# A value product with seven block products instead of eight for one of two expert pairs, its extra sums on POOL and DVE

## The reference, cut to what matters

```python
def peer_ffn(hn, w_q, sub_keys, u, v):      # hn (256, 1024); u, v (16384, 1024)
    ...                                      # top-16 experts of 8 heads per token: eidx, gate
    act = gelu(einsum('td,ted->te', xb, u[eidx])) * gate
    return einsum('te,ted->td', act, v[eidx])
```

## Time and profile before

| | us |
|---|---|
| median of 3 runs | 2187.45 (2179.83 to 2189.59) |
| the profiled execution's own time | 2180.91 |
| its span, first to last instruction | 2179.1 |
| value stage, layer 0 / layer 1 | 348.4 / 348.6 |
| mean granted TensorE clock | 0.986 of full speed |

### The profile page before, as it was taken

The page is one execution under the profiler, slowest core; times in us unless marked ns, Lnnn a source line. Parts: engine busy times, 40 slices in busy tenths (PEclk is TensorE's granted clock), DMA queues, the critical chain, the costliest instruction groups (busy, mean ns, idle before and its releaser), DMA issues.

```text
span 2179.1 us, 45295 instructions
## 1 busy us (share of the span) xinstructions
PE 2089.8 (96%) x14548; PEld 1896.7 (87%) x14548; DVE 1441.2 (66%) x3050; ACT 1314.5 (60%) x3093; POOL 388.9 (18%) x342
## 2 busy tenths in 40 slices
PE   7889899999999999999998998999999999999997
PEld 7889499999999988888788895999999998888886
DVE  5764349778887666666567633496778886666665
ACT  5530145699999655555565302556999995555554
POOL 0312007632222100000003120175322220000000
PEclk9999999999999999999999998999999999999999
DMA  5320244444444555555552102444444445555554
GB/s 210 116 78 1 97 155 165 165 171 157 156 168 157 176 192 192 192 192 192 192 189 97 59 1 98 173 174 166 162 155 170 156 155 191 194 193 192 192 192 184
DMA packets 47464, 338.82 MB, mean 155 GB/s; under 512 B 5649, under 2 KB 5777, under 8 KB 6929
## 3 DMA queue, kind: packets, MB, share of 16 engines
q1 hardware_dynamic: 47376, 337.73, 43.2%
HBM read 336.66 MB, written 1.05 MB: 155 GB/s over the span
## 4 chain that ended last, share of the span: by engine, by line
PE 85%; DVE 9%; ACT 2%; DMA 2%; issue 1%; DVEq 0%; SPq 0%; ACTq 0%; PEldq 0%
PE ps L815 11%; PE ps L814 11%; PE ps L816 11%; PE ps L784 10%; PE ps L786 9%; PE ps L785 9%; PE ps L687 3%; PE ps L407 2%; PE ps L408 2%; PE ps L409 2%; PE ps L550 2%; PE ps L564 1%; PE ps L794 1%; PE ps L795 1%; PE ps L423 1%; DVE expert_lo L1320 1%
## 5 line engine op out<-in xcount | busy, mean ns | idle before, releaser
L784 PE MATMUL ps<-h_t_hi,expert_hi 128*128 128x256 f32 x2048 | 591.3, 289 | 12.3 <-DVE expert_lo L1686 8.5
L785 PE MATMUL ps<-h_t_lo,expert_hi 128*128 128x256 f32 x2048 | 578.5, 282 | 0.0
L786 PE MATMUL ps<-h_t_hi,expert_lo 128*128 128x256 f32 x2048 | 578.2, 282 | 0.0
L1869 POOL TENSOR_TENSOR expert_lo<-w_ring,expert_hi 128x512 fp32r<-128x512 f32 x204 | 289.8, 1429 | 772.1 <-ACT expert_hi L975 770.4
L784 PEld LDWEIGHTS ps<-h_t_hi,expert_hi 128*128 128x128 f32 x2048 | 391.6, 191 | 15.6 <-ACT big L980 8.2
L814 PE MATMUL ps<-expert_hi,act_hi 128*128 128x512 f32 x1024 | 398.4, 389 | 0.0
L815 PE MATMUL ps<-expert_lo,act_hi 128*128 128x512 f32 x1024 | 398.4, 389 | 0.0
L816 PE MATMUL ps<-expert_hi,act_lo 128*128 128x512 f32 x1024 | 398.3, 389 | 0.0
L785 PEld LDWEIGHTS ps<-h_t_lo,expert_hi 128*128 128x128 f32 x2048 | 392.0, 191 | 0.0
L786 PEld LDWEIGHTS ps<-h_t_hi,expert_lo 128*128 128x128 f32 x2048 | 391.6, 191 | 0.0
L975 ACT CAST expert_hi<-w_ring 128x512 fp32r<-128x512 f32 x512 | 308.0, 614 | 98.3 <-PE ps L786 83.7
(11 more groups left out here) (294 smaller groups left out, 3279.2 us busy)
## 6 DMA issues: line engine op xcount, KB each, us to landing
w_ring<-u_t SPq DMA_DIRECT2D x128, 1024.0 KB, 4.8
w_ring<-v_t SPq DMA_DIRECT2D x128, 1024.0 KB, 4.8
w_ring<-w_in SPq DMA_DIRECT2D x32, 1024.0 KB, 4.8
w_ring<-w_q SPq DMA_DIRECT2D x16, 1024.0 KB, 4.8
w_ring<-w_out SPq DMA_DIRECT2D x8, 1024.0 KB, 4.8
big<-xconst SPq DMA_DIRECT2D x2, 1666.0 KB, 9.5
w_ring<-keys SPq DMA_DIRECT2D x2, 1024.0 KB, 4.7
big<-rows SPq DMA_DIRECT2D x2, 576.0 KB, 11.2
```

The source lines that it names most:

```text
L784: pe.matmul(o, w_hi[:, c, :], HTH[:, d, :], start=d == 0, stop=False)
L785: pe.matmul(o, w_hi[:, c, :], HTL[:, d, :], start=False, stop=False)
L786: mm = pe.matmul(o, w_lo[:, c, :], HTH[:, d, :], start=False, stop=d == DC - 1)
L1869: pool.tensor_tensor(EL[:, m % 4, :], RING[:, m // 4, (m % 4) * 512:(m % 4 + 1) * 512], EH[:, m % 4, :].bitcast(F32), ALU.subtract).then_i ...
```

## The change

Bodies 1 to 30 of each layer treat their first expert pair as a product of 2x2 blocks: the activations as A (token tile x expert tile), the values as B11, B12, B21, B22 (expert tile x column half). A Strassen-type scheme (Winograd's form) computes it with seven block products p1 to p7 instead of eight. Each is three matmuls of 128x512, as before. The second pair stays as it was and is now called c0 to c3. Body 0 and body 31 of each layer keep the old form.

The scheme needs sums of the operands: four 128x128 sums of activations (`ASUM`, POOL), and four 128x512 sums of values: T1 = B12 - B11, T2 = T3 + B11 and T4 = B21 - T2 on POOL, T3 = B22 - B12 on DVE. POOL also makes the low of the four activation sums (`ASL`). Highs are still ACT's and all other lows DVE's. There are now six buffers for highs and lows of values (four `EH`, two in `h_t_hi`, free in this stage).

The products p2, p3, p4 are added into banks 0, 1 and 2; p1, p5, p6 and p7 have banks 4 to 7. After the last body `fold` combines them with eight DVE additions of 128x512, before the four additions of before.

The loads are cut into four of 512 KB per body, each with its own semaphore. Load 0 (B11, B12) now waits for T2 of the body before, load 1 (B21, B22) for T4.

PE:

```diff
+            def v_product(name, j, bank, a_hi_t, a_lo_t, start):
+                pe.wait_ge(v_lo, v_at(name, j))
+                o, s = PS[:, bank, :], v_slot(name)
+                pe.matmul(o, a_hi_t, VH[s], start=start, stop=False, skip_group_check=True)
+                pe.matmul(o, a_hi_t, VL[s], start=False, stop=False, skip_group_check=True)
+                pe.matmul(o, a_lo_t, VH[s], start=False, stop=True, skip_group_check=True).then_inc(v_done, 1)
...
+            def v_body(j, first):
+                pe.wait_ge(a_lo, 4 * j + 1)
+                v_product("p1", j, 4, A11H, A11L, first)
+                pe.wait_ge(a_lo, 4 * j + 3)
+                v_product("p2", j, 0, A2H[:, a12], A2L[:, a12], False)
+                pe.wait_ge(s_lo, j)
+                v_product("p3", j, 1, ASH[:, s4], ASL[:, s4], False)
+                v_classic("c0", j, 0, 0)
+                v_product("p7", j, 7, ASH[:, s3], ASL[:, s3], first)
+                v_product("p6", j, 6, ASH[:, s2], ASL[:, s2], first)
+                v_product("p5", j, 5, ASH[:, s1], ASL[:, s1], first)
+                v_classic("c1", j, 0, 1)
+                v_product("p4", j, 2, A2H[:, a22], A2L[:, a22], False)
+                pe.wait_ge(a_lo, 4 * j + 4)
+                v_classic("c2", j, 1, 0)
+                v_classic("c3", j, 1, 1)
```

ACT, one body (`b_high` waits for its buffer and makes one high of 512; `left(name)` waits until PE has done that product of the body before):

```diff
+                left("p1", 1)
+                act.copy(A11H, acts(0, 0, P)).then_inc(a_hi, 1)
+                act.wait_ge(v_landed[0], 16 * (j + 1))
+                b_high("p1", B11, j, first)
+                act.wait_ge(s_made, 3 * j)
+                left("p5", 1)
+                act.copy(ASH, ASUM).then_inc(s_hi, 1)
+                act.wait_ge(v_landed[1], 16 * (j + 1))
+                b_high("p2", B21, j, first)
+                left("c1", 6)
+                act.copy(AH[:, 0, :], acts(2, 0, S)).then_inc(a_hi, 1)
+                left("p4", 1)
+                act.copy(A2H, acts(1, 0, S)).then_inc(a_hi, 1)
+                b_high("p3", B22, j, first)
+                act.wait_ge(v_landed[2], 16 * (j + 1))
+                b_high("c0", RING[:, 1, 0:512], j, first)
+                act.wait_ge(t3_made, j)
+                b_high("p7", T3, j, first)
+                act.wait_ge(t_made, 3 * j - 1)
+                b_high("p6", T2, j, first)
...
+                b_high("p5", T1, j, first)
+                b_high("c1", RING[:, 1, 512:1024], j, first)
+                act.wait_ge(t_made, 3 * j)
+                b_high("p4", T4, j, first)
...
```

DVE, one body (`b_low` waits for the high and makes one low of 512):

```diff
+                a_low(1, A11L, 0, 0, P, A11H)
+                b_low("p1", B11, j)
+                b_low("p2", B21, j)
+                dve.tensor_tensor(T3, B22, B12, ALU.subtract).then_inc(t3_made, 1)
+                a_low(2, AL[:, 0, :], 2, 0, S, AH[:, 0, :])
+                a_low(3, A2L, 1, 0, S, A2H)
+                b_low("p3", B22, j)
...
+            def fold():
...
+                dve.wait_ge(folded, 1)
+                plus(T1, PS[:, 6, :])
+                plus(x11, PS[:, 4, :])
+                plus(x22, PS[:, 5, :])
...
```

POOL, one body:

```diff
+                    pool.tensor_copy(ATOP, both)
+                    pool.tensor_tensor(s3, acts(0, 0), acts(0, 1), ALU.subtract)
+                    pool.tensor_tensor(s1, acts(0, 1), acts(1, 1), ALU.add).then_inc(s_made, 1)
+                    pool.wait_ge(s_made, 3 * j - 2)
+                    pool.tensor_tensor(s2, s1, ATOP[:, 0, :], ALU.subtract).then_inc(s_made, 1)
+                    pool.wait_ge(s_made, 3 * j - 1)
+                    pool.tensor_tensor(s4, ATOP[:, 1, :], s2, ALU.subtract).then_inc(s_made, 1)
+                    pool.wait_ge(v_landed[0], 16 * (j + 1))
...
+                    pool.tensor_tensor(T1, B12, B11, ALU.subtract).then_inc(t_made, 1)
+                    pool.wait_ge(s_hi, j)
+                    pool.tensor_tensor(ASL, ASUM, ASH.bitcast(F32), ALU.subtract).then_inc(s_lo, 1)
+                    pool.wait_ge(t3_made, j)
+                    pool.tensor_tensor(T2, T3, B11, ALU.add).then_inc(t_made, 1)
+                    pool.wait_ge(v_lo, v_at("p3", j))
+                    pool.wait_ge(t_made, 3 * j - 1)
+                    pool.tensor_tensor(T4, B21, T2, ALU.subtract).then_inc(t_made, 1)
```

SP:

```diff
+                with sp.Fori(2, N_BODY) as j:
+                    sp.wait_ge(t_made, 3 * j - 4)
+                    load_v(0, j)
+                    sp.wait_ge(t_made, 3 * j - 3)
+                    load_v(1, j)
+                    sp.wait_ge(v_lo, v_at("c1", j - 1))
+                    load_v(2, j)
+                    sp.wait_ge(v_lo, v_at("c3", j - 1))
+                    load_v(3, j)
```

More of the change, by code:

```diff
@@ L363, in _ @@
                     sp.wait_ge(*u_lows_made(4 * i + 3, N_BODY - 1, False))
[L364 to L368, removed]
+                    for c in range(2):
+                        load_v(2 * i + c, 0)
+                for c in range(4):
+                    sp.wait_ge(v_lo, 2 * c + 2)
+                    load_v(c, 1)
+                with sp.Fori(2, N_BODY) as j:
[7 more added lines that the diff above has]
+                    load_v(3, j)
                 for i in range(2):
-                    sp.wait_ge(v_lo, 252 + 4 * i)
+                    sp.wait_ge(v_lo, V_ALL - 4 + 4 * i)
                 first_loads(L - 1)
@@ L891, in _ @@
                 for m in range(8):
[L892 to L896, removed]
+                    v_half(m, 0, True, 0)
+                v_body(1, True)
+                with pe.Fori(2, N_BODY - 1) as j:
+                    v_body(j, False)
+                for m in range(8):
+                    v_half(m, N_BODY - 1, False, V_ALL - 8)
+                pe.wait_ge(v_done, V_ALL)
                 pe.sem_inc(arrived, 1)
@@ new lines, in a_split, with b_high @@
+                if first and e == 2:
+                    act.wait_ge(u_mul, 2 + 128 - LATE)
+                if e >= 2:
+                    act.wait_ge(v_done, 2 * e - 2 if first else V_ALL - 10 + 2 * e)
+                elif not first:
+                    act.wait_ge(v_done, v_at(("c1", "c3")[e], j - 1))
+                act.copy(AH[:, e % 2, :], ACTS[:, 4 * j + e, :]).then_inc(a_hi, 1)
+            def b_high(name, src, j, first):
+                act.wait_ge(v_done, slot_left(name, j, first))
+                act.copy(VH[v_slot(name)], src).then_inc(v_hi, 1)
@@ L1264, in _ @@
                     v_split(m, 0, True)
[L1265 to L1270, removed]
+                v_body(1, True)
+                with act.Fori(2, N_BODY - 1) as j:
+                    v_body(j, False)
+                for m in range(8):
+                    if m % 2 == 0:
+                        a_split(m // 2, N_BODY - 1, False)
+                    v_split(m, N_BODY - 1, False)
+                act.wait_ge(v_done, v_at("p5", N_BODY - 2))
+                act.wait_ge(v_lo, v_at("p4", N_BODY - 2))
+                act.copy(T1, PS[:, 4, :]).then_inc(folded, 1)
+                act.wait_ge(v_hi, V_ALL)
                 for t in range(NT):
@@ L1842, in _ @@
                     v_lows(m, 0)
[L1843 to L1847, removed]
+                v_body(1, True)
+                with dve.Fori(2, N_BODY - 1) as j:
+                    v_body(j, False)
+                for m in range(8):
+                    if m % 2 == 0:
+                        a_lows(m // 2, N_BODY - 1)
+                    v_lows(m, V_ALL - 8)
+                fold()
                 for f in range(2):
-                    dve.wait_ge(v_done, 255 + f)
+                    dve.wait_ge(v_done, V_ALL - 1 + f)
                     for t in range(NT):
@@ L1954, in _, with v_body, acts @@
                         u_lows(m, j)
+                def v_body(j, first):
+                    def acts(e, t):
+                        return ACTS[:, bass.ds(4 * j + e, 1) if not first else slice(4 * j + e, 4 * j + e + 1), t * P:(t + 1) * P].rearrange("p a n -> p (a n)")
+                    both = ACTS[:, bass.ds(4 * j, 2) if not first else slice(4 * j, 4 * j + 2), 0:P]
+                    s1, s3, s2, s4 = (ASUM[:, i * P:(i + 1) * P] for i in range(4))
+                    pool.tensor_copy(ATOP, both)
[6 more added lines that the diff above has]
+                    pool.wait_ge(v_landed[0], 16 * (j + 1))
+                    if not first:
+                        pool.wait_ge(v_lo, v_at("p5", j - 1))
+                    pool.tensor_tensor(T1, B12, B11, ALU.subtract).then_inc(t_made, 1)
[6 more added lines that the diff above has]
+                    pool.tensor_tensor(T4, B21, T2, ALU.subtract).then_inc(t_made, 1)
+                pool.wait_ge(u_mul, 2 + 128 - LATE)
+                pool.wait_ge(quad_done, N_QUAD)
+                v_body(1, True)
+                with pool.Fori(2, N_BODY - 1) as j:
+                    v_body(j, False)
                 pool.sem_inc(arrived, 1)
```

105 lines of the change are left out of this document (90 added, 15 removed).

## The result

The changed kernel takes 2382.18 us (median of 4 runs, 2377.09 to 2386.04), the kernel before 2188.52 us (4 runs): a ratio of 1.0892, 95% interval 1.0852 to 1.0931. It is slower. The profiled execution of the changed kernel took 2378.86 us, 198.0 more than the 2180.91 of before. The forecast was 2399, range 2270 to 2490.

The account below looks back on a forecast made before the run. PE bounded the kernel before; in the change, DVE and POOL excluding each other would. 2180.9 + 204.6 (bodies) + 7.2 (tail) = 2392.7 us, as a median 2399, since the earlier median lies 6.5 above the profiled execution; range 2270 to 2490.

Parts of the forecast that it names:

- What binds: Value stage: DVE operations reading two SBUF tensors and POOL's SBUF reads exclude each other, so their times add, 8.4 + 7.1 us.
- The body: One value-stage body, bodies 1 to 30 of each layer: 14.3 us against 10.89 before, +204.6 us in all; chance 0.72.
- A hand-over: Switch between DVE and POOL in a body: saves 0.13 us, at most 9 times, taking 15.5 to 14.3 us.
- POOL's small sums: Four 128-wide activation sums per body on POOL: 0.4 us each, 1.6 us in all.
- My lower end: Low end for a body: DVE at 0.47 us per wide operation (6.3 in all) plus POOL 6.6, together 12.9 us.
- The rule of whole instructions: DVE and POOL in a body: port lock held for whole instructions, giving 15.5 us a body, 2465 us in total.
- The tail: After each layer's last body: the fold's eight DVE additions delay the final four by 3.6 us, 7.2 in all.
- The load chain and the waits: Value stage: chain through sums and half-size loads takes 9.0 to 10.0 us, costed at nothing; as binding rival, chance 0.03.
- PE does not stay the bound: Rival in the value stage: DVE and POOL overlap, PE stays the bound at 10.2 us a body, 2154 us; chance 0.10.
- The partial collision: Rival: POOL holds DVE up for only part of its instruction, 11 to 12.5 us a body, 2200 to 2290; chance 0.07.
- The clock: Rival: gaps in PE lower TensorE's clock; at a mean of 0.62, 16.5 us a body, 2531 in all; chance 0.08.
- The signs: Value stage: PE busy about 71%, DVE lows near 0.9 us, POOL's wide operations 1.5 or more, stage near 451 us.

Follow-up runs that it names:

- pool_writes_only: Changed kernel with POOL's value-stage sums replaced by fills that read nothing, all waits and signals kept: 2150.62 us.
- dve_every_second: Kernel before with seven products only in every second body, all sums on DVE, fold spread over the last body: 2346.76 us, ratio 1.0742.
- the two-of-three pattern: Kernel before with seven products in two of three bodies, all sums on DVE, fold spread over the last body: 2223.71 us, ratio 1.0173.
- the new order: Every-second-body form with mapped buffers, and activation lows before sums, second-pair products early, PE's and ACT's queues matched: 2164.52 us, ratio 0.9907.

## Why the prediction was right

**What binds.** Right, and shown: DVE and POOL exclude each other. POOL's reads turned into writes remove the loss entirely, and the work moved from POOL to DVE removes 139 us of it. The subtractions in the kernel before slow DVE with nothing else changed.

**The body.** Forecast 14.3 us (12.9 to 15.9), measured 14.07. Two terms were off, and they partly cancel. A hand-over saves more than the 0.13 us that I took for each of nine: the rows of after give 1.27 - 1.10 = 0.17 for the wide operations, 0.46 - 0.27 = 0.19 for the small ones and about 0.2 for the copy, some 1.6 us in all and not 1.2. POOL's small sums, for which no row stood before, cost more: the first two of the stage, which run alone, take 0.46 us each against my 0.4 (the copy takes 0.40, as I took it), 0.24 more for the four. With the measured terms, 8.4 of DVE + 4 x 1.10 + 4 x 0.27 + 0.2 for the copy = 14.1. The difference of 0.23 us over 60 bodies is 14 us, nearly all that the forecast lies above the result.

**A misread row.** The row from which I took the 0.13 doesn't show it. POOL's 1.74 counts from POOL's own start, which lies 0.13 behind DVE's. From DVE's start at 409.72 to POOL's end at 411.59 it is 1.87, the plain sum. The stretch at 1169 us did show a saving, 4.73 against 4.94, and the changed kernel shows one. So that I subtracted a hand-over was right, and that its size came out near was luck. Without any saving the forecast would have been 15.5 a body. My lower end was also added up wrongly: 12 x 0.47 and the narrow operations in proportion are 6.6, not 6.3, so it should be 13.2. The result lies inside either way.

**The rule of whole instructions.** The Trainium skill ("SBUF — State Buffer", SBUF: two separate sides) has the port pair held for the whole instruction. The lock is borne out by every run that tests it here; the figure that the rule gives to the letter (15.5 us a body, 2465 in all) is not: in the changed kernel the pair takes 1.70, not 1.87.

**The tail.** Forecast 3.6 us a layer, measured 3.1: the eight additions start some 0.60 us apart, not 0.66. No run isolates this term; it is read from the rows alone.

**The sum.** 60 x (14.07 - 10.89) = 190.8, and 2 x 3.1, on 2180.91 give 2377.9; the profiled execution took 2378.86.

**The load chain and the waits.** Costed at nothing, and pool_writes_only, which keeps them all, has PE without a gap at a body of 10.2 us. The landing is 3.8 us, the lower of my two.

**The rivals.** PE does not stay the bound. The partial collision comes true only for the small operations, which cost DVE 0.27 of their 0.46 us; a wide one costs 1.10 of 1.27, and the body is far above that rival's 11 to 12.5. The clock is at 1.00 (2.4 GHz) in the stage, so that rival did not come.

**The signs.** The stage to PE's last matmul takes 443.1 us (forecast near 451), and the final additions stand behind 4.83 us (forecast some 5). Of POOL's wide operations three show 1.67 to 1.75 us, but T2 only 1.38, which is under the 1.5 that I named. One sign was badly chosen: PE's busy share is 84% in the body (11.77 of 14.07), not 71%. By cadence it works 45 x 0.227 = 10.2 of 14.07, 73%, but after each gap the recorded durations of pipelined matmuls fill part of it.

## What to carry to other kernels

Before work goes to POOL to relieve DVE, look at the operands: if DVE's operations read two tensors in SBUF and POOL's read SBUF, the two queues nearly add up, and here DVE lost 5.7 us a body for work that it does itself in 3.2. Where DVE has slack, a few POOL reads spread out at its idle times are nearly free and the same in a burst are not. A saving on the engine that binds is worth only what its suppliers can follow: here half of the saving, with the buffers mapped so that no product takes the one just left and with the operands that PE needs next ahead of the sums, beats the whole.

## What was not expected of the hardware

- A burst costs more than its sum. Three POOL subtractions in a row cost 1.32 us a body and the same three spread out 0.11. The mechanism (few buffers, so no lead and no catching up) is argued from the rows; more buffers in the kernel before weren't tried.
- POOL's fills are free for DVE: lows at 688 ns beside fills of 1278 ns.
- Gaps in PE do not by themselves lower the clock. In the changed kernel PE pauses once a body for 1.5 us, and several times for up to 0.5, at a granted clock of 1.00. In dve_every_second two gaps, 1.43 and 2.79 us, lie between 908 and 913.3 us, and the clock falls and comes back (columns as in the earlier trace rows). The prediction said that a busy PE is at 2.4 GHz in every full stretch; here PE is busy for all of 914 to 918 us at a mean of 0.72, and the clock is back at 1.00 from 918:

```profile
909.00:911.00 2.00, 0.96 (x3) 0.48 (x3) 2.00 (x4) 2.00 (x6) 0.00 (x0) 1.00 0.00 0
911.00:914.00 3.00, 0.77 (x2) 0.68 (x3) 3.00 (x7) 2.08 (x5) 0.00 (x0) 0.81 0.00 1
914.00:918.00 4.00, 4.00 (x15) 3.15 (x14) 4.00 (x8) 1.87 (x4) 0.00 (x0) 0.72 0.78 261
918.00:923.00 5.00, 5.00 (x24) 4.14 (x23) 2.88 (x6) 2.39 (x5) 0.00 (x0) 1.00 0.57 183
```

Left open: whether a low with only one input in SBUF would be free beside POOL's reads, and whether the two-of-three pattern would also win with the new order; neither was tried. On the first there is a hint in the kernel before: beside the POOL low of 409.85 to 411.59 us DVE makes operations that read one tensor of SBUF and one of PSUM, and they take 0.44 and 0.45 us, as the next ones behind POOL's end do (0.44):

```profile
410.70 0.45 DVE L1648 COPY_PREDICATED h_t<-ps,big 128x256 f32<-128x256 uint32 x1
```
